# q and k projected by tokens, their norms taken along the row, and the convolution's sums and low parts on GpSimd

## What is computed

```python
def hybrid_mixer(h, w_in, q_norm_g, k_norm_g, rel_bias, w_conv, b_conv, g_attn_out, g_conv_out, w_out):
    q, k, v, xc, gate_b, gate_c = jnp.split(h @ w_in, [...], axis=-1)      # six parts of 512 columns
    q = rms_norm(q.reshape(B, S, N_HEADS, HEAD_DIM), q_norm_g)             # 8 heads of 64
    k = rms_norm(k.reshape(B, S, N_HEADS, HEAD_DIM), k_norm_g)
    v = v.reshape(B, S, N_HEADS, HEAD_DIM)
    y_attn = chunked_rel_attention(q, k, v, rel_bias).reshape(B, S, D_ATTN)
    y_conv = gate_b * causal_depthwise_conv(gate_c * xc, w_conv, b_conv)
    y = jnp.concatenate([rms_norm(y_attn, g_attn_out), rms_norm(y_conv, g_conv_out)], axis=-1)
    return y @ w_out
```

## Time and profile before

| | us |
|---|---|
| median of 3 runs | 1870.15 |
| the three runs | 1862.39, 1870.15, 1871.12 |
| the profiled execution | 1869.57 |
| its span in the profile | 1867.8 |

### The profile page before, as it was taken

The page is one execution under the profiler, slowest core; times in us unless marked ns, Lnnn a source line. Parts: engine busy times, 40 slices in busy tenths (PEclk is TensorE's granted clock), DMA queues, the critical chain, the costliest instruction groups (busy, mean ns, idle before and its releaser), DMA issues.

```text
span 1867.8 us, 21528 instructions
## 1 busy us (share of the span) xinstructions
PE 1797.4 (96%) x8384; PEld 1482.4 (79%) x8384; DVE 1149.9 (62%) x1346; ACT 667.5 (36%) x859; POOL 489.0 (26%) x287
## 2 busy tenths in 40 slices
PE   3989999999999989999999999999999999999997
PEld 3778888888788778877788878878888888888875
DVE  6978776667787573247552468667445444468756
ACT  3443333333343443224333144333323333333442
POOL 1146445654100001202223030114434443310000
PEclk9999999999999999998999999999999999999998
DMA  9035665466856323231232320402333223585633
GB/s 361 23 121 193 200 212 163 164 203 229 317 203 236 94 74 102 82 115 46 74 127 74 102 88 1 132 26 87 106 107 124 84 95 107 177 313 195 231 90 110
DMA packets 84659, 260.98 MB, mean 140 GB/s; under 512 B 8160, under 2 KB 8160, under 8 KB 83040
## 3 DMA queue, kind: packets, MB, share of 16 engines
q1 hardware_dynamic: 79968, 251.49, 40.0%
q10 hardware_dynamic: 4608, 8.39, 1.2%
HBM read 211.09 MB, written 48.76 MB: 139 GB/s over the span
## 4 chain that ended last, share of the span: by engine, by line
PE 84%; DVE 6%; issue 5%; ACT 2%; DMA 1%; POOL 1%; SPq 0%; POOLq 0%; DVEq 0%; ACTq 0%
PE pair L2047 20%; PE pair L2048 20%; PE pair L2049 20%; PE pair L2041 6%; PE pair L2043 6%; PE pair L2042 6%; PE pair L2384 3%; PE pair L2350 2%; PE pair L2365 1%; DMA raw<-hs 1%; PE pair L2294 1%; DVE ada L1436 1%; DVE w_lo L1352 1%; DVE cb L1497 1%; DMA x<-xT 0%
## 5 line engine op out<-in xcount | busy, mean ns | idle before, releaser
L2047 PE MATMUL pair<-cb,w_hi 128*128 128x512 f32 x864 | 338.5, 392 | 7.9 <-DVE w_lo L1352 4.9
L2048 PE MATMUL pair<-cb,w_hi 128*128 128x512 f32 x864 | 337.9, 391 | 0.0
L2049 PE MATMUL pair<-cb,w_lo 128*128 128x512 f32 x864 | 337.7, 391 | 0.0
L2047 PE MATMUL pair<-h_hi,w_hi 128*128 128x512 f32 x824 | 322.6, 392 | 11.9 <-DVE w_lo L1352 9.2
L2048 PE MATMUL pair<-h_lo,w_hi 128*128 128x512 f32 x824 | 322.1, 391 | 0.0
L2049 PE MATMUL pair<-h_hi,w_lo 128*128 128x512 f32 x824 | 322.0, 391 | 0.0
L2047 PEld LDWEIGHTS pair<-cb,w_hi 128*128 128x128 f32 x864 | 163.4, 189 | 43.2 <-DVE w_lo L1352 5.8
L2047 PEld LDWEIGHTS pair<-h_hi,w_hi 128*128 128x128 f32 x824 | 155.6, 189 | 45.4 <-DVE w_lo L1352 9.6
L2049 PEld LDWEIGHTS pair<-cb,w_lo 128*128 128x128 f32 x864 | 163.3, 189 | 34.1
L2048 PEld LDWEIGHTS pair<-cb,w_hi 128*128 128x128 f32 x864 | 163.3, 189 | 33.8
L2048 PEld LDWEIGHTS pair<-h_lo,w_hi 128*128 128x128 f32 x824 | 155.6, 189 | 32.4
(11 more groups left out here) (184 smaller groups left out, 3070.3 us busy)
## 6 DMA issues: line engine op xcount, KB each, us to landing
raw<-hs SPq DMA_DIRECT2D x70, 512.0 KB, 3.8
ada_w<-w_ada SPq DMA_DIRECT2D x55, 512.0 KB, 3.7
raw<-w_mix SPq DMA_DIRECT2D x48, 512.0 KB, 3.5
hs<-tt SPq DMA_DIRECT2D x20, 1024.0 KB, 6.4
a<-w_f1o SPq DMA_DIRECT2D x30, 512.0 KB, 6.5
a<-w_f2o SPq DMA_DIRECT2D x30, 512.0 KB, 6.0
ga<-w_f1i SPq DMA_DIRECT2D x22, 512.0 KB, 4.3
ua<-w_f1i SPq DMA_DIRECT2D x22, 512.0 KB, 4.4
```

The costliest lines, as they stand in the source:

```text
L2047: nc.tensor.matmul(dst, lh, rh, start=first, stop=False, skip_group_check=True)
L2048: nc.tensor.matmul(dst, lh, rl, start=False, stop=False, skip_group_check=True)
L2049: return nc.tensor.matmul(dst, ll, rh, start=False, stop=False, skip_group_check=True)
```

## The change

- q and k are computed like v, by tokens: four chunks of q weights into banks 0 to 3, then four of k into banks 4 to 7 (`by_token`). A bank then holds 128 tokens x 8 heads of 64 features.
- The norm runs along the row: ScalarE squares a bank, VectorE sums each 64 values (`tensor_reduce`) and adds epsilon, GpSimd takes the power of 128x8 values, VectorE multiplies the bank by it (broadcast) into `q_norm` (`qrow` or `ytok`). TensorE transposes this tile (four transposes, `qk_turn`) back into its own bank, one turn behind each of the last three k chunks and the first five convolution chunks. ScalarE copies out with the gain: `q_out`, in reverse token order, and `k_out`. `qk_stats`, `qk_spread`, `reverse_q` and the `q_rev` buffers are gone; scores read `q_sb`.
- In the attention loop GpSimd does the four sums of squares (`conv_add`) and the four low parts (`conv_lo`) of a mixer instead of VectorE. In mixer 0 `OUT_SPLITS` puts the first four `w_out` splits at units 6, 7, 10, 12 instead of 0, 1, 4, 6. GpSimd's order is written anew around them.

```diff
-        OUT_SPLITS = [{0: 0, 1: 1, 4: 2, 6: 3, 20: 4, 24: 5, 29: 6}, {1: 0, 2: 1, 7: 2, 10: 3}]
+        OUT_SPLITS = [{6: 0, 7: 1, 10: 2, 12: 3, 20: 4, 24: 5, 29: 6}, {1: 0, 2: 1, 7: 2, 10: 3}]
...
+                for i in range(8):
+                    pool.wait_ge(qvar_done, 8 * mx + i + 1)
+                    o = i * HEADS
+                    nc.gpsimd.tensor_tensor(qinv[:, o:o + HEADS], qvar[:, o:o + HEADS], mhalf[:], ALU.pow)\
+                        .then_inc(qpow_done, 1)
...
+                def conv_add(t):
+
+                    n = NORM_CONV[mx]
+                    pool.wait_ge(sq_done, norm_sq(n) + t + 1)
+                    pool.wait_ge(acc_done, norm_acc(n) + t + 1)
+                    nc.gpsimd.tensor_tensor(acc[:], acc[:], sq[:], ALU.add).then_inc(acc_done, 1)
+
+                def conv_lo(ct):
+
+                    pool.wait_ge(y_hi_done, KA * mx + ct + 1)
+                    a = (KA + ct) * T
+                    nc.gpsimd.tensor_tensor(col(y_lo, a, T), tmp[:], col(y_hi, a, T).bitcast(F32),
+                                            ALU.subtract).then_inc(yc_ready, 1)
+
+                for t in range(KA):
+                    conv_add(t)
                 if mx == 0:
+                    power(NORM_CONV[mx])
+                    out_lo(0)
+                    conv_lo(0)
+                    out_lo(1)
+                    conv_lo(1)
+                    y_power(0)
+                    conv_lo(2)
+                    out_lo(2)
+                    conv_lo(3)
+                    out_lo(3)
+                    y_power(1)
...
+                def qk_square(i):
+
+                    g = 8 * mx + i
+                    act.wait_ge(w_used, b + (MIX_K if i < TT else MIX_CONV))
+                    act.wait_ge(qsum_done, g) if g else None
+                    nc.scalar.activation(qsq[:], bank[i][:], ACT.Square).then_inc(qsq_done, 1)
+
+                def q_out(i):
+
+                    act.wait_ge(qt_mm, 8 * mx + i + 1)
+                    src = bass.AP(bank[i].tensor, bank[i].offset + P - 1, [list(bank[i].ap[0]), [P, KA], [-1, P]])
+                    dst = col(q_sb, i * T, T).rearrange("p (t c) -> p t c", t=KA)
+                    nc.scalar.activation(dst, src, ACT.Identity, scale=qg[:, 0:1]).then_inc(qk_done, 1)
...
+                def qk_mean(i):
+
+                    g = 8 * mx + i
+                    dve.wait_ge(qsq_done, g + 1)
+                    o = i * HEADS
+                    nc.vector.tensor_reduce(qsum[:, o:o + HEADS], qsq[:].rearrange("p (h d) -> p h d", h=HEADS),
+                                            mybir.AxisListType.X, ALU.add).then_inc(qsum_done, 1)
+                    dve.wait_ge(qsum_done, g + 1)
+                    nc.vector.tensor_scalar(qvar[:, o:o + HEADS], qsum[:, o:o + HEADS], 1.0 / HD, EPS,
+                                            ALU.mult, ALU.add).then_inc(qvar_done, 1)
...
+                for c in range(4):
+                    mix_lo(b + MIX_K + c)
+                qk_mean(0)
+                qk_mean(1)
+                mix_lo(b + MIX_CONV)
+                qk_mean(2)
+                qk_scale(0)
+                qk_mean(3)
+                mix_lo(b + MIX_CONV + 1)
+                qk_scale(1)
...
-                    if 0 <= s - 1 < KA:
-                        add_square(NORM_CONV[mx], s - 1)
                     if s == CONV_STATS[mx]:
                         mean(NORM_CONV[mx])
-                    if s - 1 in CONV_SPLIT[mx]:
-                        conv_second(CONV_SPLIT[mx].index(s - 1))
...
+                for c in range(4):
+                    by_token(b + MIX_K, c, 4)
+                    if c:
+                        qk_turn(c - 1)
                 for c in range(8):
                     if c < 4:
-                        pe.wait_ge(qk_done, 8 * mx + 5 + c)
+                        pe.wait_ge(qk_done, 8 * mx + c + 1)
                     else:
                         pe.wait_ge(cg_done, KA * mx + c - 3)
                     projection(b + MIX_CONV + c, c % 4)
-                    if c == 0:
-                        qk_stats(7)
-                        qk_spread(6)
-                    if c == 1:
-                        qk_spread(7)
+                    if c < 5:
+                        qk_turn(c + 3)
```

More of the change, by code:

```diff
@@ new lines, in _ @@
+                mix_hi(b + MIX_CONV + 1)
+                q_out(0)
+                mix_hi(b + MIX_CONV + 2)
+                q_out(1)
+                mix_hi(b + MIX_CONV + 3)
+                q_out(2)
+                qk_square(4)
+                qk_square(5)
+                mix_hi(b + MIX_CONV + 4)
+                q_out(3)
+                conv_copy(0)
+                qk_square(6)
+                qk_square(7)
+                mix_hi(b + MIX_CONV + 5)
+                k_out(0)
+                conv_copy(1)
@@ new lines, in _ @@
+                for c in range(4):
[8 more added lines that the diff above has]
+                qk_scale(1)
+                mix_lo(b + MIX_CONV + 2)
+                qk_scale(2)
+                mix_lo(b + MIX_CONV + 3)
+                qk_scale(3)
+                qk_mean(4)
+                qk_mean(5)
@@ L2285, in projection @@
                     mm.then_inc(w_used, 1)
-                def qk_stats(u):
-                    g = 8 * mx + u
-                    pe.wait_ge(qsq_done, g + 1)
-                    pe.wait_ge(qvar_done, g) if g else None
-                    pe.wait_ge(v_done, TT * (mx + 1)) if u == 0 else None
-                    for t in range(TT):
-                        mm = nc.tensor.matmul(bank[4][:, 2 * t:2 * t + 2], qsq[:, t * P:(t + 1) * P], one2[:, 1:3],
-                                              start=True, stop=True)
-                    mm.then_inc(qst_mm, 1)
```

231 lines of the change are left out of this document (96 added, 135 removed).

## The result

The changed kernel takes 1856.07 us (median; 1854.08 to 1856.53) against 1870.51 us (1862.39 to 1871.12) for the kernel before: a ratio of 0.993 with a 95% interval of 0.991 to 0.995. It is 14.4 us shorter, where 23.5 were forecast; the time lies in the range, at the place of the first rival.

The account below looks back on a forecast made before the run. TensorE, busy 96% of the span, was taken as the bound. -13.4 - 1.5 - 1.0 + 1.0 - 0.3 - 8.0 = -23.2 on the profiled 1869.57 gave 1846.4, as a median 1847.0 us; range 1842 to 1860.

Parts of the forecast that it names:

- first rival: First mixer's attention loop: the clock still falls there, 1855.0 us; chance 0.30.
- Statistics gone, -13.4: q and k projections, both mixers: TensorE loses statistics of 0.84 us a tile, 16 tiles, -13.4 us.
- The turns: TensorE before the 16 qk_turn: no waits, 0 us; slack 1.5 us at the first, near 2.9 later.
- The old waits, -1.5 and -1.0: First mixer's attention loop: TensorE's wait at 850 goes, -1.5 us; those at 873.92 and behind lose 1.0 us.
- the new one, +1.0: First mixer's loop, before norm_stats: TensorE waits for GpSimd's fourth add, +1.0 us (bounds 0 and 1.6).
- GpSimd beside VectorE: Eight exposed VectorE steps a mixer, each late by 0 to 1.05 us beside GpSimd; 0 in the sum.
- The second rival: Attention loops: VectorE's two-input steps held up beside GpSimd hold the scores; +5 in the second mixer, 1862 us; chance 0.07.
- The clock, -8.0: First mixer's attention loop: the fall to half speed, 17.0 us long, goes; -8.0 us (bounds 0 and 8.5).
- the second mixer's attention: TensorE is the bound there; its few waits give -0.3 us (0 to -1).
- the chain of adds: Second mixer's attention: ScalarE squares and GpSimd adds have 4 us of room before the statistics, 0 us.
- The likeliest case: Whole kernel: the forecast itself, 1847.0 us, alone 1843 to 1850; chance 0.55.

Follow-up runs that it names:

- e3: Late splits: changed kernel, GpSimd's out_lo 1 and 2 after the last conv_lo in mixer 0, ScalarE's splits 2, 3 at units 15, 18; 1849.66 us, ratio 0.9885.
- e1: q and k alone: changed kernel with the convolution's adds and low parts back on VectorE, old OUT_SPLITS and GpSimd order; 1855.12 us, ratio 0.9915.
- e11: e1 again without an edit, for a second profile; 1856.01 us, ratio 0.9932.
- e5: Splits alone: kernel before with only mixer 0's out_lo moved, adds and low parts of the convolution staying on VectorE; 1870.96 us, ratio 1.0004.
- e2: Loop's part alone: kernel before with the change's OUT_SPLITS, and conv_add and conv_lo on GpSimd; 1871.48 us, ratio 1.0006.
- e7: e2 made again with reverse_q(2) put ahead of out_lo on GpSimd; 1870.20 us, ratio 0.9997.
- e8: Kernel before, without an edit, for a second profile; one execution, 1874.92 us.
- e10: e3 again without an edit, timed beside the changed kernel on one chip; 1851.11 us, ratio 0.9895.

## Why the prediction was right or wrong

*Statistics gone, -13.4: right.* D lost 6.84 us and A, taken without the fall at 694 (157.11 and 157.14 in `e3` and `e1` against 163.95), 6.84: -13.7 in all, and 0.59 us between chunks.

*The turns: right.* No TensorE wait stands before any of the 16, and the sum over 64 elements took 682 ns where 0.7 was taken.

*The old waits, -1.5 and -1.0, and the new one, +1.0: right in kind, for the wrong sum.* The 1.50 us is gone, for the reason given, as the splits alone show. The new wait for the add is 0.55 us. GpSimd's four starts are the foretold 2.1 us apart (838.87 to 845.09); its add took 1.27 us, not 1.40, and TensorE came 0.3 us later after the first square than was reckoned.

*GpSimd beside VectorE, "0 in the sum": the first step that failed.* The prediction knew the mechanism and priced each meeting at up to 1.05 us; it then let VectorE's idle time pay for it all. But the step stands in front of scores that TensorE awaits, and a step that is late by 1.48 us in the first mixer made a wait of 1.86. At full clock the loop takes 33.6 us in its old form (`e1`, `e11`, whose waits are the old ones), 34.0 to 34.2 in the changed one (37.34 less half of 6.6; 35.87 less half of 3.4), and 31.8 with late splits (35.26 and 35.24, less half of 6.8). The forecast said 1.5 us less than the old form. It is 0.5 more as the change was made, and 1.8 less once two `out_lo` are moved out of the way: in its waits, the forecast's loop is the one with late splits. The price was low too: 1.03 and 1.48 us above the 0.75 here, and up to 1.95 in `e5`, where `conv_first` came just behind the start of the second of two. The Trainium skill, page "SBUF — State Buffer", section "SBUF: two separate sides", says of a VectorE instruction with two SBUF inputs and a GpSimd instruction that reads SBUF that the later one is blocked for the whole of the other. By that, this case's rows agree: `conv_first` at 857.06 ended 0.54 us after GpSimd's 2.37 us, and the one of 2.70 us 0.55 after the end of the 4.67. The second rival was this mechanism, but its price for the second mixer (+5) was wrong: its four `conv_first` take 0.75 us each, from 1110.40 on, and the last `out_lo` had ended at 1102.28. E moved by -0.04 in all.

*The clock, -8.0: the step that cost most.* The size was right (8.1 for the old fall), and that the old fall would go at its place was right; that no other would come was not. In this profile B has 6.6 us at half clock instead of 17.0 (4.8 us gained), C holds 1.66 of a fall's tail and A 1.62 of the one at 694: 1.5 us gained of 8.0. In the second profile of the same kernel B alone gained 6.4 (8.1 less half of 3.4), nothing was lost in C, and the 1.6 at 694 was lost again. The prediction's remark that VectorE is busy 1.0 to 1.1 of 2 us "in the stretches shown" holds for the two from 852 and 866, not for the one from 850, where it is at 2.00.

*The sum.* Forecast -23.2, profile -15.5. The 7.7 us between them are, to 0.1: 6.5 from the clock, 2.0 from VectorE beside GpSimd (-1.5 forecast, +0.5 found), 0.3 from the second mixer's attention (q and k alone gave -0.4 there, and the chain of adds, which was to cost 0, took it back), less 0.3 from the projections and 0.7 outside the stretches.

*The rivals.* The first (the clock still falls in the first attention loop; 1855.0 us) is what happened in time, but with its reason in the second one: the waits ahead of the falls are VectorE's behind GpSimd, not the new one at `norm_stats`. With late splits the fall does stand behind that one (0.55 us), as the first rival has it. A chance of 0.07 for a mechanism whose every part was in the rows, and that the prediction priced as nothing, was too little. The likeliest case, 1843 to 1850, was missed; the range held the time because the first rival was inside it. That it came within 1.1 us of that rival's 1855.0 is in part luck: the same kernel's second profile took 1851.24, with one fall fewer.

## What to carry to other kernels

Work moved from VectorE to GpSimd, or only moved in time on GpSimd, can be paid for by a VectorE step with two SBUF inputs that then meets it: list those steps with their times, and put GpSimd's long reads (here 2.4 us each) where none of them stands ahead of something that TensorE awaits. Removing TensorE work where TensorE is the bound gave its full count, twice 6.8 us, while the gain of a removed wait was taken back by the next one: at full clock the convolution's part, as it was made, costs about 1 us (0.5 in B, 0.4 to 0.6 in E) against q and k alone. And a fall of the clock is not removed with one wait: credit it in part, and keep its whole price in the range.

## What the runs showed of the hardware

- A VectorE step with two SBUF inputs (128x512) that started while GpSimd's subtraction of 128x1024 (2.35 to 2.4 us) ran ended 0.54 or 0.55 us after the end of that instruction, whenever it had started: the adds at 846.92 and 849.78 in the kernel before, `conv_first` at 857.06 and 866.24 in the changed one, 864.20 in `e2`, 873.04 in `e7`, 860.06 in `e5`, `conv_second` at 868.30 and 873.73 there. They took 0.92 to 2.70 us, 0.68 to 0.75 otherwise.
- Where the first fall of the clock in this loop stands was the same in both profiles of each kernel, within 2 us: at 850 and 852 in the kernel before, at 862 in the changed one, at 846 and 848 with late splits, nowhere in that loop with q and k alone. How much time at half clock the loop then has was the same twice with late splits (6.8 us), but not in the kernel before (17.0 and 30.7 us) nor in the changed one (6.6 and 3.4, by a second fall that came once). The wait ahead doesn't decide alone: 1.50 us with a fall in the kernel before, 1.48 without one in `e1` and `e11`; 1.04 us with a fall in the changed kernel's first profile, 1.03 without one in its second; 0.55 us without one in the changed kernel, and with one in the late splits. What decides is not shown here.
- A fall costs half of its length while it is short (8.1 for 17.0; 1.47 for 3.2 us more), and less when long: 13.7 us more at half clock cost the loop 4.28. Ahead of a wait for something else it can cost nothing: the fall at 678 in `e1` left A at 157.14 (157.11 in `e3`, without one).
- The fall at 694 comes and goes in the same kernel (not in the first profile of before, but in `e8`; not in `e3`, but in `e10`), and is worth 1.6 us. Differences of a few us between single executions of this kernel are of that kind: the slower executions of q and k alone (1854 to 1858 against 1849) have the lower mean clock.
